# RWKV recurrence on one core: forward level products with block-diagonal weights of two heads, backward ones by single heads

## What is computed

```
def step(S, inp):
    r_t, w_t, a_t, b_t, k_t, v_t = inp
    sa = jnp.einsum('bhvk,bhk->bhv', S, a_t)
    S = S * w_t[:, :, None, :] + sa[..., None] * b_t[:, :, None, :] + v_t[..., None] * k_t[:, :, None, :]
    return S, jnp.einsum('bhvk,bhk->bhv', S, r_t)
```

## Time and profile before

| what | value |
|---|---|
| median of 3 runs | 2594.16 us (2587.97 to 2595.68) |
| the profiled execution, own time | 2594.5 us |
| its span | 2592.7 us |
| mean granted TensorE clock | 0.941 |
| TensorE busy | 2253.1 us (87%) |
| DVE / ACT / POOL busy | 1159.0 / 707.5 / 392.0 us |
| the recurrence, layer 1 and layer 2 | 186.8 us and 183.8 us |

### The profile page before, as it was taken

One profiled execution on the slowest core, in us unless ns is written; L12 is line 12 of the kernel. 1 busy time (PEld: TensorE's weight loads), 2 busy tenths in 40 slices (PEclk: granted clock), 3 DMA queues, 4 the chain that ended last, 5 costly groups with the idle time before them and its releaser, 6 DMA issues. The chain is left out here.

```text
span 2592.7 us, 49039 instructions
## 1 busy us (share of the span) xinstructions
PE 2253.1 (87%) x19954; PEld 1492.5 (58%) x19954; DVE 1159.0 (45%) x2561; ACT 707.5 (27%) x1666; POOL 392.0 (15%) x465
## 2 busy tenths in 40 slices
PE   6999989887789998899889679999888878897785
PEld 3444455547754444466556568877657767554453
DVE  3877765575542114532212563244675542522113
ACT  2011155464441002132222120024454430222220
POOL 0000000044520001132222000000133400222210
PEclk8999999999999998999999889999889999899998
DMA  9455401210016103699988733313210033999994
GB/s 379 195 211 238 168 33 43 79 46 5 4 52 259 73 1 126 263 384 388 372 348 319 297 143 113 115 67 98 98 40 4 4 128 129 355 414 390 382 377 180
DMA packets 80368, 474.39 MB, mean 183 GB/s; under 512 B 17296, under 2 KB 29200, under 8 KB 51728
## 3 DMA queue, kind: packets, MB, share of 16 engines
q1 hardware_dynamic: 55280, 419.82, 41.3%
q0 software_dynamic: 24864, 51.43, 5.2%
HBM read 439.99 MB, written 61.08 MB: 193 GB/s over the span
## 5 line engine op out<-in xcount | busy, mean ns | idle before, releaser
L2883 PE MATMUL xp_psG<-moe_ring,rt_xt 128*64 128x256 f32 (+1 forms) x2048 | 324.5, 402 | 42.5 <-DMA moe_ring<-in_moe 41.9
L2883 PEld LDWEIGHTS xp_psG<-moe_ring,rt_xt 128*64 128x64 f32 (+1 forms) x2048 | 225.4, 161 | 119.6 <-issue 48.2
L599 PE MATMUL win_ps<-h,win_ring 128*128 128x512 f32 x512 | 226.2, 600 | 5.4 <-PEq L292 5.4
L659 DVE SCALAR_TENSOR_TENSOR mod_acc<-ada_ring,cv_silu,mod_acc 128x512 f32<-128x512 f32 x280 | 197.9, 748 | 10.8 <-issue 0.4
L3140 DVE TENSOR_TENSOR rt_sg<-rt_sg,xp_psG 128x128 f32<-128x128 f32 x84 | 24.2, 288 | 332.3 <-ACT rt_sg L2957 332.3
L599 PEld LDWEIGHTS win_ps<-h,win_ring 128*128 128x128 f32 x512 | 97.0, 192 | 125.6 <-issue 125.6
L2904 PE MATMUL xp_psY<-moe_ring,rt_aT 128*64 128x512 f32 (+1 forms) x512 | 162.1, 602 | 4.0 <-DVE rt_aT L3147 4.0
L2192 PE MATMUL sc_ps<-sc_NT,sc_XI 64*64 64x64 f32 x2560 | 112.9, 235 | 23.3 <-issue 18.9
L1274 POOL MEMSET ml_w<- 128x1536 f32 x4 | 5.4, 1376 | 764.9 <-POOLq L973 764.9
L2187 PE MATMUL sc_ps<-sc_XI,sc_NT 64*64 64x64 f32 x2048 | 100.7, 226 | 22.1 <-issue 16.6
L2073 DVE TENSOR_TENSOR sc_XI<-sc_ps,cst 128x256 f32<-128x256 f32 x160 | 67.5, 422 | 107.9 <-PE sc_ps L2192 107.0
(11 more groups left out here) (537 smaller groups left out, 4293.4 us busy)
## 6 DMA issues: line engine op xcount, KB each, us to landing
moe_ring<-in_moe SPq DMA_DIRECT2D x128, 1536.0 KB, 14.3
ada_ring<-in_ada SPq DMA_DIRECT2D x22, 2048.0 KB, 15.1
win_ring<-in_win SPq DMA_DIRECT2D x20, 2048.0 KB, 7.8
cb_yg<-y_rows SPq DMA_DIRECT2D x16, 1024.0 KB, 11.6
mg_ring<-in_mg SPq DMA_DIRECT2D x16, 768.0 KB, 4.4
mg_wo<-in_wo SPq DMA_DIRECT2D x2, 4096.0 KB, 14.5
pr<-y_rows SPq DMA_DIRECT2D x8, 1024.0 KB, 18.4
ml_gate_ring<-in_mg SPq DMA_DIRECT2D x12, 512.0 KB, 3.7
```

The lines of the kernel that those rows point to most:

```text
L599: last = pe.matmul(ps[:, n % NB, first(n):T], ring[:, j % 2, c, m * P:(m + 1) * P], h[:, c, first(n):T], start=c == 0, stop=c == KD - 1)
L659: last = dve.scalar_tensor_tensor(out=acc[:, a % 2, s], in0=aring[:, a % 3, c], scalar=weight, in1=acc[:, a % 2, s], op0=ALU.mult, op1=ALU ...
L2883: last = pe.matmul(psG[at:at + m, u % 2, 0:2 * P].rearrange("p (q n) -> p q n", q=2), xt[:, u % 2, c, at:at + m], ring[:, slot, c:2 * KD:K ...
```

## The change

The data keeps its place in the partitions: no `place` and no `across` any more. `NT` becomes block-diagonal, [128, 4, 2, 64], with zeros off the diagonal (POOL clears it once), in two buffers.

- Level products m = 1 to 4: the forward one multiplies a pair of heads at once, with 128x128 weights, four per direction instead of eight 64x64. The backward one stays at eight single heads, each at its own quarter (r, r), and is issued first.
- Its result is copied in halves of 64 partitions: for direction 0 both by ACT (`evens`, `odds`), for direction 1 one by ACT and one by DVE (`odds`).
- Level 0 (`first_level`) runs on partitions 0 to 63 alone; `X0` holds 8 heads in 64 partitions. The second matrices come in two halves, of even and odd heads.
- The turning of `hat` is four transposes of 128x128 per direction. `matrices` are eight products of 64x128 with 128 columns instead of sixteen of 64x64. They stand after level 4 of the step before instead of after level 5.
- The unit matrix is added by TensorE: a product of `ident` and the right side (256 columns) goes ahead of the corrections in `psU`, one of `ident` and S ahead of the state products in `psS`; DVE has one operation per state instead of two.
- Three exponentials of 256 columns and a small one become two.

The core of the diff:

```diff
-                def copied(d, n, m):
-                    w(act, d, "nn", n, m + 1)
-                    act.activation(NT[d][:], psWT[d], ACT.Copy).then_inc(sem[d]["wtout"].sem, 1)
+                def evens(d, n, m):
+                    w(act, d, "back", n, m + 1)
+                    act.activation(NT[m % 2][d][0:HD, :, 0], psWT[d][0:HD], ACT.Copy).then_inc(sem[d]["evens"].sem, 1)
...
+                blocks = pn[:, NK_T + 2:NK_T + 6]
+                pool.memset(blocks, 0.0)
...
                     for h, hp, r in heads:
-                        o = h % 2
-                        for a, q in enumerate((r, HD - r)):
-                            pe.matmul(psA[d][q:q + HD, o, hp], hat[n % 2][d][r:r + HD, hp, a],
-                                      ra[n % 2][d][r:r + HD, hp].rearrange("p a n -> p (a n)"), start=True, stop=True)
+                        last = pe.matmul(psA[d][:, h % 2, hp], hat[n % 2][d][r:r + HD, hp].rearrange("p a n -> p (a n)"),
+                                         ra[n % 2][d][r:r + HD, hp].rearrange("p a n -> p (a n)"), start=True, stop=True)
...
                 def level(d, n, m):
...
+                    if m == 5 and n + 1 < NST:
+                        second_matrices(d, n + 1, 0)
+                    wt = NT[(m - 1) % 2][d]
+                    for h, hp, r in heads:
+                        last = pe.matmul(psWT[d][r:r + HD, hp], XI[d][r:r + HD, hp], wt[r:r + HD, hp, h % 2],
+                                         start=True, stop=True)
+                    last.then_inc(sem[d]["back"].sem, 1)
                     if m < 5:
-                        for hp in range(KC // 2):
-                            forward(hp)
-                            last = backward(hp + KC // 2, psWT[d][:, hp + KC // 2])
-                        last.then_inc(sem[d]["across"].sem, 1)
-                        between(d, n, m)
-                        w(pe, d, "across", n, m + 1)
...
+                        for hp in range(KC):
+                            last = pe.matmul(psW[d][:, hp], wt[:, hp], XI[d][:, hp], start=True, stop=True)
+                        last.then_inc(sem[d]["nn"].sem, 1)
+
+                def token_major(d, n):
+                    w(pe, d, "state", n)
+                    for hp in range(KC):
+                        last = pe.transpose(psBK[d][:, hp * P:(hp + 1) * P],
+                                            hat[n % 2][d][:, hp].rearrange("p a n -> p (a n)"), k.cst("ident"))
...
+                    pe.matmul(psU[d], k.cst("ident"), rhs[d][:], start=True, stop=False)
+                    for hp in range(KC):
+                        last = pe.matmul(psU[d][:, hp], NT[1][d][:, hp], rhs[d][:, hp], start=False, stop=hp == KC - 1)
...
+                        pe.matmul(psS[d], k.cst("ident"), S[d][:], start=True, stop=False)
...
                 def step(n):
-                    for m in range(1, 6):
+                    for m in range(1, 5):
                         for d in range(2):
                             level(d, n, m)
+                            if m == 1:
+                                token_major(d, n)
+                            elif m == 2:
+                                side_of_state(d, n)
+                            elif m == 3:
+                                side_of_values(d, n)
+                            elif n + 1 < NST:
+                                matrices(d, n + 1)
                     for d in range(2):
+                        level(d, n, 5)
                         if n + 1 < NST:
-                            matrices(d, n + 1)
-                        corrections(d, n)
+                            second_matrices(d, n + 1, 1)
```

More of the change, by code:

```diff
@@ L1824, in stage_rwkv_scan @@
 def stage_rwkv_scan(nc, k, l, pr, pn, sg, aa, kk, ka, y, h):
[L1834 to L1837, removed]
+    names = ("exps", "feats", "queries", "mats", "masked", "seconds", "turned", "tok", "xi", "back", "nn", "evens", "odds",
+             "rstate", "r", "rout", "u", "uout", "ystate", "s", "rows", "yout", "state")
+    per_step = dict(exps=1, feats=1, queries=1, mats=1, masked=1, seconds=2, turned=1, tok=1, xi=6, back=6, nn=5, evens=6,
+                    odds=6, rstate=1, r=1, rout=1, u=1, uout=1, ystate=1, s=1, rows=1, yout=1, state=1)
     sem = [dict(zip(names, k.signals(*[f"scan{d}_{n}" for n in names]))) for d in range(2)]
@@ L1897, in w @@
             s = sem[d][name]
-            eng.wait_ge(s.sem, s.at(count + (n - (outs.start if name == "rows" else 0)) * per_step[name]))
+            eng.wait_ge(s.sem, s.at(count + (n - (outs.start if name in ("rows", "ystate") else 0)) * per_step[name]))
         def y_read(n):
@@ L1948, in step @@
                     for m in range(1, 5):
[L1949 to L1956, removed]
+                        evens(0, n, m)
+                        odds(0, n, m)
+                        if m == 2:
+                            token_major(0, n)
+                        if m == 4:
+                            right_side(1, n)
+                        if n == 0 and m == 1:
+                            exponentials(0, 1)
+                            exponentials(1, 1)
+                        evens(1, n, m)
+                        if m == 2:
+                            token_major(1, n)
+                        if m == 3:
+                            right_side(0, n)
                     if n + 2 < NST:
                         exponentials(0, n + 2)
+                    evens(0, n, 5)
+                    odds(0, n, 5)
+                    evens(1, n, 5)
                     for d in range(2):
@@ L1977, in _ @@
                     values(j)
-                for d in range(2):
-                    copied(d, 0, 0)
+                evens(0, 0, 0)
+                odds(0, 0, 0)
+                evens(1, 0, 0)
                 for n in range(NST):
@@ new lines, in level @@
+                    wt = NT[(m - 1) % 2][d]
+                    for h, hp, r in heads:
+                        last = pe.matmul(psWT[d][r:r + HD, hp], XI[d][r:r + HD, hp], wt[r:r + HD, hp, h % 2],
+                                         start=True, stop=True)
+                    last.then_inc(sem[d]["back"].sem, 1)
+                    if m < 5:
+                        for hp in range(KC):
+                            last = pe.matmul(psW[d][:, hp], wt[:, hp], XI[d][:, hp], start=True, stop=True)
+                        last.then_inc(sem[d]["nn"].sem, 1)
@@ new lines, in token_major, with side_of_state @@
+                def token_major(d, n):
[3 more added lines that the diff above has]
+                                            hat[n % 2][d][:, hp].rearrange("p a n -> p (a n)"), k.cst("ident"))
+                    last.then_inc(sem[d]["turned"].sem, 1)
+                def side_of_state(d, n):
+                    w(pe, d, "state", n)
+                    pe.wait_ge(sem[d]["yout"].sem, sem[d]["yout"].at(y_read(n)))
+                    for h, hp, r in heads:
+                        last = pe.matmul(psR[d][r:r + HD, hp], ra[n % 2][d][r:r + HD, hp, 1], S[d][r:r + HD, hp],
+                                         start=hp == 0, stop=False)
+                    last.then_inc(sem[d]["rstate"].sem, 1)
@@ L2265, in rows_of_state, with side_of_values @@
+                def side_of_values(d, n):
+                    w(pe, d, "rstate", n)
+                    for h, hp, r in heads:
+                        last = pe.matmul(psR[d][r:r + HD, hp], M[n % 2][d][HD:P, h % 2, hp, L:P],
+                                         uv[HD:P, chunk(d, n), h], start=False, stop=hp == KC - 1)
+                    last.then_inc(sem[d]["r"].sem, 1)
                 def rows_of_state(d, n):
```

268 lines of the change are left out of this document (116 added, 152 removed).

## The result

| | before | after |
|---|---|---|
| median | 2594.92 us (4 runs, 2587.97 to 2598.2) | 2766.07 us (4 runs, 2757.73 to 2768.8) |
| profiled execution, span | 2592.7 us | 2765.1 us |
| recurrence, layer 1 | 186.7 us | 268.9 us |
| recurrence, layer 2 | 183.5 us | 272.0 us |

The ratio is 1.0658, with a 95% interval of 1.0626 to 1.069. Forecast were 2720 us and a range up to 2762, so the direction is right, and the time lies 4 us outside the range. The two recurrences grew by 82.2 and 88.5 us in the profiled executions; all the rest of the program by 1.7.

The account below looks back on a forecast made before the run. Before was taken as bound by TensorE's instruction count, after by its work: 30.6 us a full step, adding 61.7 us (layer 1), 61.5 (layer 2) and 2.2 at layer 2's start, +125.4 to 2720 us; range 2650 to 2762, 80%.

Parts of the forecast that it names:

- The bound of before: Recurrence before the change: the number of TensorE instructions, not their work, sets the pace, at 15.84 ns a row.
- The end of that bound: Recurrence after the change: 34 to 36 instruction packets in each layer and hardly any idling for "issue".
- The sum of a step: One full step after the change: products 26.3 us, changes of array form 3.4, new wait 0.9, together 30.6.
- The forward product: Levels 1 to 4: eight full-weight records per direction, 0.90 us, where eight small ones took about 0.25.
- The wait: Between levels 4 and 5: TensorE waits for direction 1's key query from DVE, 0.9 us a step.
- a change of form: TensorE switching between 64x64 tiles and the full array: 27 a step at 0.125 us, 3.4 us.
- the matrices: Matrices of a step: two row tiles at once, 0.90 us a direction; 1.8 if one after the other.
- I price it from rows at the full clock: TensorE work of the changed step: durations taken from profile rows at full clock, 26.3 us a step.
- the granted clock, 0.94 and 0.88 before, nearer to 1: Both recurrences: the profile after the change would show a granted clock nearer to 1.
- Slower still: Rival: matrices don't overlap (+25 us), another wait at the step's end (+15), 2760 us; above 2762: 6%.
- Weights that beat at 0.057 us: Rival: full-weight records as fast as small ones, 4.4 us less a step, 2652 us; result of 2602 to 2650: 6%.
- the count stays the bound: Rival: instruction count still sets the pace after the change, 17.2 us a step, 2515 us; chance 5%.

Follow-up runs that it names:

- single heads: Changed kernel with the forward level product back at eight single heads (64x64 weights) per direction: 2662.56 us, ratio 1.0266.
- queries earlier: Changed kernel with direction 1's queries for the next step one level earlier on DVE: 2737.9 us, ratio 1.0543.
- reordered levels: Changed kernel with the queries moved earlier and, per level, both directions' backward products before both forward ones: 2708.38 us, ratio 1.0441.

## Why the prediction was off

- **The bound of before** was read rightly: 112 rows fewer at about equal work made the kernel 26 us faster (28 expected), of which some 1.4 us a step are the count's; the rest goes with before's half clock. The page of the Trainium skill named in the forecast ("Runtime: NRT & Kernel Launch", Instruction fetch mechanics) calls the crossing mostly hidden; the run disagrees. The rows of before and after were counted rightly too (352 products need six "other" ones of eight, not five).
- **The end of that bound** too: 34 packets, no "issue" waits, and 128 rows more cost nothing in the run with single heads.
- **The sum of a step**, 26.3 + 3.4 + 0.9 = 30.6, measured 31.03. The forward product was right (1.03 us for 0.90 and a change of form). The wait was mis-sized: 1.14 us for 0.9, the query beside GpSimd. That the rest, 29.7, came out so near to the 29.81 of the run without the wait is in part luck: a change of form costs 0.15 and not 0.125, the matrices 1.09 us a direction (641.67 to 642.76) and not 0.90, together some 1.0 us a step, and other terms, which no run separates, were as much too dear. At full clock (but for its first 6.8 us) layer 1 is 252.9 us, 66.2 over before, against 61.7 forecast. In layer 2 I take the second execution, 267.5, less 16 for its stretch: 251.5, 68.0 over before, against 63.7. This is 8.8 of the 47.0 us that were missed.
- **The step that failed** is "I price it from rows at the full clock", with "the granted clock, 0.94 and 0.88 before, nearer to 1". The first profile after shows 0.92 and 0.90: 37.5 us at 1.2 GHz near the start of both recurrences, 16.0 us in layer 1 and 20.5 in layer 2 (272.0 less 251.5; it has three short pieces at half besides, 1.5 us each). With the 1.7 outside the recurrences the terms add up to what the profiled executions differ by: 125.4 + 8.8 + 36.5 + 1.7 = 172.4. They must, since 8.8 and 36.5 are differences of measured times; what backs them is that 20.5 is also 16.0 and three times 1.5. The second execution, with one long stretch less, took 2754.87 us and lies inside the range: the 4 us that the median lies outside are less than the 12 us by which two executions of the same kernel differ.
- **Before had half clock as well**, but in pieces of 3.4 to 10.2 us: 23.5 and 43.6 us in its two recurrences, against 44.0 and 53.8 in the changed kernel (6.7 and 43.8 in its second execution). I took its average as a price that the new kernel would not pay. It pays some 0.43 us for each: 1.5 for a piece of 3.4 (a step without output of 30.9 us in place of 29.4), 16.0 for one of 37.5. One long piece per layer belonged in the range: 2762 should have been some 30 us higher.
- **The rivals.** "Slower still" came nearest in time and was wrong in mechanism: the matrices overlap in pairs, and no second wait arose. Weights that beat at 0.057 us and "the count stays the bound" are refuted.

What brings on the long stretch stays open. The longest piece at half clock in each recurrence, us:

| kernel | layer 1 | layer 2 |
|---|---|---|
| changed | 37.5 | 37.5 |
| changed, second execution | 6.8 | 37.5 |
| queries earlier | 34.1 | 51.2 |
| four products of 512 columns added | 6.8 | 13.7 |
| 64 small products added | 6.8 | 13.7 |
| 16 small products added | 6.8 | 47.8 |
| 64 in four pieces added | 6.8 | 20.5 |
| single heads | 6.8 | 13.7 |
| reordered levels | 6.8 | 17.1 |

With the changed kernel's levels it was there in 5 of 6 recurrences without added products and in 1 of 8 with them, and the ratios of those four runs (1.0599 to 1.0631) lie under the changed kernel's 1.0658 though they do more. So an effect of the added work isn't excluded; one profile of each can't show it, and 13.7 and 17.1 us with single heads or reordered levels are as little proof that the alternation of forms is to blame.

## What to carry to other kernels

Count instructions where a packed engine idles for "issue": with cheap products their number is the bound, and four transposes for 16 small products a direction gave 1.1%. Fewer but larger instructions win only while their work stays below the pace of the fetches; here, with fp32 and full weights, it did not. And once a stretch is bound by TensorE's work, put its time at half clock into the range, by the longest pieces that profiles show, and profile the same kernel twice before explaining 10 us by an edit.

## What the hardware did that was not expected

- TensorE, busy for 36.54 of 37.50 us (in the run with earlier queries for 34.00 of 34.00), stayed at 1.2 GHz; the same instructions ran at 2.4 GHz in another execution. That this is TensorE's real pace shows in the forward group: 1.89 us there, 1.03 at full clock. The Trainium skill ("TensorE: Matmul & The Clock Gate", What's actually happening) says that activity releases the throttle. Here the measurement decides: it did not for 37.5 us.
- A change between 64x64 tiles and the full array cost 0.15 us (1.35 us for nine a step), on top of the usual distance from record to record; the forecast had 0.125.
- The key query, a DVE operation on 128x256, took 0.71 us in place of 0.41 while GpSimd's L1997 and L1998 ran beside it.
